# Two-layer hybrid decoder on one core: the first layer's S5 b matrices loaded later, their products moved to GpSimd, and three small reorderings

## What is computed

```
h = rms_norm(x);  proj = h @ w_in            # 1024 x 6424, split by columns
mixer A: S5 diagonal state space, 32 groups x 16 channels, 64 complex states
    bb = f * b           (f from lambda and step; b: 32 x 64 x 16, real and imaginary)
    x = u @ bb;  h = scan(a, x);  y = Re(c @ h) + d*u;  gelu, glu
mixer B: compressed / selected / window attention with rotary positions (rope)
mixer C: stick-breaking attention (softplus, running sums, exp)
x = x + (sum of gates * (mixer @ w_branch)) @ w_out
x = x + (silu(conv3(h @ up_gate)) * conv3(h @ up_value)) @ w_down
```

## Time and profile before

| | |
|---|---|
| median of 3 runs | 948.28 us (947.02 to 948.35) |
| the profiled execution | 950.34 us, its span 948.6 us, mean granted clock 0.996 |
| PE busy | 925.0 us, 98% of the span |
| DVE, ACT, POOL busy | 708.3, 592.2 and 289.2 us |
| idle before PE's work, the largest by releaser | DVE wl L1733 5.7 us, DMA at the start 3.2 us, DVE wl (at L959) 2.4 us |

### The profile page before, as it was taken

The page is one execution under the profiler, slowest core; times in us unless marked ns, Lnnn a source line. Parts: engine busy times, 40 slices in busy tenths (PEclk is TensorE's granted clock), DMA queues, the critical chain, the costliest instruction groups (busy, mean ns, idle before and its releaser), DMA issues.

```text
span 948.6 us, 16008 instructions
## 1 busy us (share of the span) xinstructions
PE 925.0 (98%) x5839; PEld 776.7 (82%) x5839; DVE 708.3 (75%) x1131; ACT 592.2 (62%) x956; POOL 289.2 (30%) x226
## 2 busy tenths in 40 slices
PE   8899999999999999999999999999999999999997
PEld 6889777777778888888879987777787788888886
DVE  6799967665667887898864977766657687777777
ACT  7445776768455765666665467677664566566655
POOL 0433324351420568467101413443316001010010
PEclk9999999999999999999999999999999999999999
DMA  9993433453554755556449844433645456556551
GB/s 221 247 269 98 147 123 132 132 150 129 167 176 138 219 192 193 177 185 213 139 123 264 233 154 134 133 117 106 180 131 178 133 178 207 193 177 205 191 179 45
DMA packets 139559, 159.09 MB, mean 168 GB/s; under 512 B 17153, under 2 KB 106089, under 8 KB 139498
## 3 DMA queue, kind: packets, MB, share of 16 engines
q1 hardware_dynamic: 137960, 156.44, 53.6%
q10 hardware_dynamic: 1538, 1.84, 0.7%
HBM read 154.33 MB, written 1.05 MB: 164 GB/s over the span
## 4 chain that ended last, share of the span: by engine, by line
PE 78%; DVE 9%; ACT 4%; SPq 3%; DMA 2%; issue 2%; ACTq 1%; POOL 0%; DVEq 0%; PEldq 0%; POOLq 0%
PE pj L801 57%; PE bX L801 7%; PE bA L801 6%; PE bB L801 4%; DVE wl L1733 3%; DMA ring<-in_w_in 2%; PE pj L1069 1%; ACT wh L1390 1%; SPq L618 1%; PE pj L1165 1%; SPq L671 1%; DVE gate L1758 1%; DVE s5a L1960 1%; DVE h L1765 1%; SPq L615 1%
## 5 line engine op out<-in xcount | busy, mean ns | idle before, releaser
L1733 DVE TENSOR_TENSOR wl<-ring,wh 128x1024 fp32r<-128x1024 f32 (+1 forms) x276 | 361.4, 1311 | 96.0 <-ACT wh L1390 94.8
L1390 ACT ACTIVATE wh<-ring 128x1024 fp32r<-128x1024 f32 (+1 forms) x276 | 288.2, 1045 | 154.4 <-PE pj L801 112.0
L801 PE MATMUL pj<-h,wh 128*128 128x256 f32 (+1 forms) x1376 | 296.6, 339 | 6.0 <-DVE wl L1733 5.0
L801 PE MATMUL pj<-wh,h 128*128 128x512 f32 (+1 forms) x832 | 259.6, 394 | 2.4 <-DVE h L1765 0.8
L801 PEld LDWEIGHTS pj<-h,wh 128*128 128x128 f32 x1376 | 230.6, 191 | 32.8 <-issue 7.0
L801 PE MATMUL pj<-h,wl 128*128 128x256 f32 x1024 | 189.0, 283 | 0.0
L801 PEld LDWEIGHTS pj<-wh,h 128*128 128x128 f32 x832 | 148.4, 188 | 41.5 <-issue 7.3
L801 PEld LDWEIGHTS pj<-h,wl 128*128 128x128 f32 x1024 | 157.6, 191 | 6.5
L801 PE MATMUL pj<-wl,h 128*128 128x512 f32 (+1 forms) x416 | 159.7, 384 | 0.0
L2422 POOL TENSOR_TENSOR work<-work 128x512 f32<-128x512 f32 x20 | 41.1, 2056 | 260.8 <-DVE work L2198 199.0
L801 PEld LDWEIGHTS pj<-wl,h 128*128 128x128 f32 x416 | 78.1, 188 | 16.3
(11 more groups left out here) (305 smaller groups left out, 1228.8 us busy)
## 6 DMA issues: line engine op xcount, KB each, us to landing
ring<-in_ffn_w_up SPq DMA_DIRECT2D x44, 1024.0 KB, 5.1
ring<-in_w_in SPq DMA_DIRECT2D x40, 1024.0 KB, 5.1
ring<-in_ffn_w_down SPq DMA_DIRECT2D x22, 1024.0 KB, 5.0
ring<-in_w_in SPq DMA_DIRECT2D x16, 512.0 KB, 5.5
ring<-in_w_branch SPq DMA_DIRECT2D x8, 1024.0 KB, 5.3
ring<-in_w_out SPq DMA_DIRECT2D x8, 1024.0 KB, 5.1
ring<-in_w_branch SPq DMA_DIRECT2D x8, 512.0 KB, 6.5
ring<-in_w_in SPq DMA_DIRECT2D x8, 256.0 KB, 3.4
```

The source lines that it names most:

```text
L801: return nc.tensor.matmul(o, a, b, start=start, stop=stop, skip_group_check=True)
L1390: A(dst, src, ACT.Copy).then_inc(w_hi.sem, 1)
L1733: TT(dst, src, hi.bitcast(F32), ALU.subtract).then_inc(w_lo.sem, 1)
```

## The change

- **Loading.** The two b matrices leave `load_mats` and get a semaphore of their own. In the first layer they are issued behind chunk 6. The rows stay behind chunk 5. What waited for six matrices now waits for four.
- **Making bb.** DVE's `s5_b` goes. POOL first does all four rope cosines, then `spread_b` (which waits for the b matrices), the products, the sums and the second spread, in one run. `s5_c`, `s5_b` and `s5_direct` on PE, the copies out on ACT, `s5_diagonal` on DVE and `s5_carried` on POOL move one slot earlier.
- **Last feed-forward step.** `ah` and `al` are made in two halves of 256 columns, with a semaphore count each; PE waits for the second before its second piece.
- **Start of the second layer.** The split of piece 1 moves behind the second `x_down` and `turned_lo`.
- **Slot 35.** The third softplus moves between the two gate copies.

```diff
-S5_C, S5_B = 2, (3, 4)
+S5_C, S5_B = 1, (2, 3)
+B_LATE, ROWS_LATE = 6, 5
...
+            def load_b(l):
+                for r, w in enumerate((ssm_b_re, ssm_b_im)):
+                    sp.dma_start(bnat[:, r], row(w, l).rearrange("l (t w) p i -> (w p) (l t) i", w=2))\
+                        .then_inc(b_in.sem, b_in.up(16))
+
             def load_mats(l):
-                for r, w in enumerate((ssm_b_re, ssm_b_im)):
-                    mat_in(bnat[:, r], row(w, l).rearrange("l (t w) p i -> (w p) (l t) i", w=2))
...
                 for i in range(5, C_FFN):
                     load(l, i)
-                    if l == 0 and i == 5:
+                    if l == 0 and i == B_LATE:
+                        load_b(0)
+                    if l == 0 and i == ROWS_LATE:
                         sp.wait_ge(setup.sem, 5)
                         load_rows(0)
...
                         if t == 0 and k:
+                            pe.wait_ge(a_split.sem, a_split.at(l, STEPS + 1))
                             pe.wait_ge(w_lo.sem, w_lo.at(l, s + 2))
...
-                    A(ah[:, :], aT[:, cc % 2, :], ACT.Copy).then_inc(a_hi.sem, 1)
-                    a_hi.made += times
+                    for c in ((slice(0, T), slice(T, 2 * T)) if cc == STEPS - 1 else (slice(0, 2 * T),)):
+                        A(ah[:, c], aT[:, cc % 2, c], ACT.Copy).then_inc(a_hi.sem, 1)
+                        a_hi.made += times
...
                     x_down(l - 1, 1, 0)
                     turned_lo(l, 1, 0, 0, 0)
-                    split_lo(l, 1)
                     x_down(l - 1, 1, 1)
                     turned_lo(l, 2, 0, 1, JC)
+                    split_lo(l, 1)
...
                 split_lo(l, 8)
-                if l == 0:
-                    s5_b()
                 split_lo(l, 9)
...
                             nc.vector.tensor_copy(gates[:, 0, t, half(1)], pj[t][:, :])\
                                 .then_inc(unit_out[n % 2].sem, unit_out[n % 2].up())
+                            if t == 0:
+                                sb_softplus(SB_P[q + 1])
+                    if q in SB_P and q != GATE_LATE + 1:
+                        sb_softplus(SB_P[q])
...
             for l in range(DEPTH):
                 cos_b = kon[:, K_COS:K_COS + T].rearrange("p (o t) -> p o t", o=1)
-                if l == 0:
-                    g.wait_ge(b_made.sem, 1)
-                    g.wait_ge(consts_in.sem, 16)
-                    spread(bb, l, 0).then_inc(bx_ready.sem, bx_ready.up())
-                    products_ab(l)
-                    sums_ab()
                 for n, dst in enumerate((kr[:, 0:2, :], kr[:, 2:3, :], qr[:, 0:2, :], qr[:, 2:4, :])):
...
-                    if l == 0 and n == 1:
-                        spread_ab(l)
+
+                if l == 0:
+                    spread_b(l)
+                    products_ab(l)
+                    sums_ab()
+                    spread_ab(l)
```

More of the change, by code:

```diff
@@ L400, in build @@
         rows_in = sem("rows_in", 16 * 11)
-        mats_in = sem("mats_in", 16 * 6)
+        b_in = sem("b_in", 16 * 2)
+        mats_in = sem("mats_in", 16 * 4)
         params_free = sem("params_free", 1, 1)
@@ L431, in build @@
         bx_ready = sem("bx_ready", 2)
-        b_made = sem("b_made")
         cx_ready = sem("cx_ready", 2)
@@ L492, in build @@
         a_ready = sem("a_ready", STEPS)
-        a_hi = sem("a_hi", STEPS)
-        a_split = sem("a_split", STEPS, 2)
+        a_hi = sem("a_hi", STEPS + 1)
+        a_split = sem("a_split", STEPS + 1, 2)
         down_done = sem("down_done", 4)
@@ L774, in _ @@
                     load_rows(l + 1)
+                    load_b(l + 1)
                     load_mats(l + 1)
@@ L1393, in spread_c @@
             def spread_c():
-                a.wait_ge(mats_in.sem, mats_in.at(0, 16 * 6))
+                a.wait_ge(mats_in.sem, mats_in.at(0, 16 * 4))
                 a.wait_ge(consts_in.sem, 16)
@@ L1880, in table @@
                     stepped(TT(tn[:, :, n:2 * n], tn[:, :, n:2 * n], turned_both[:, 0], ALU.add))
[L1882 to L1889, removed]
             for l in range(DEPTH):
@@ L2084, in s5_scan, with sb_softplus @@
                     ins.then_inc(g5_ready.sem, g5_ready.up())
+                def sb_softplus(k):
+                    v.wait_ge(z_ln.sem, z_ln.at(l, k + 1))
+                    if k:
+                        v.wait_ge(r_done.sem, r_done.at(l, k))
+                    for e in range(2):
+                        ins = STT(sbp[:, e, 0:384], (bA, bB)[e][:, 0:384], 0.0, sbw[k % 2][:, e, 0:384], ALU.max, ALU.add)
+                    ins.then_inc(z_sp.sem, z_sp.up())
                 if l:
@@ L2232, in ffn_step @@
                         split_lo(l, ffn_piece(1) + 3)
-                    v.wait_ge(a_hi.sem, a_hi.at(l, cc + 1) + turn * 2)
-                    TT(al[:, :], aT[:, cc % 2, :], ah[:, :].bitcast(F32), ALU.subtract).then_inc(a_split.sem, 1)
-                    a_split.made += times
+                    for n, c in enumerate((slice(0, T), slice(T, 2 * T)) if cc == STEPS - 1 else (slice(0, 2 * T),)):
+                        v.wait_ge(a_hi.sem, a_hi.at(l, cc + 1 + n) + turn * 2)
+                        TT(al[:, c], aT[:, cc % 2, c], ah[:, c].bitcast(F32), ALU.subtract).then_inc(a_split.sem, 1)
+                        a_split.made += times
                     if cc == STEPS - 1:
@@ L2270, in spread_c @@
             def spread_c(l):
-                g.wait_ge(mats_in.sem, mats_in.at(l, 16 * 6))
+                g.wait_ge(mats_in.sem, mats_in.at(l, 16 * 4))
                 for c, mask in enumerate((K_PAR, K_NPAR)):
@@ L2291, in spread_b @@
                 g.wait_ge(turns_ready.sem, 1)
+                g.wait_ge(b_in.sem, b_in.at(l, 16 * 2))
                 TT(bb[:, 0], bnat[:, 0], f, ALU.mult)
```

## The result

The changed kernel takes 950.32 us (median of 11 runs, 948.93 to 951.94); the kernel before, run beside it, 948.18 (11 runs, 947.02 to 949.77). The ratio is 1.0022, 95% interval 1.0012 to 1.0031: some 2 us slower, which is little, but the interval does not hold 1. Forecast were 949.3 us, 1.0 us slower, and a range of 944.0 to 953.5. The profiled execution took 951.42 us, its span 949.7; it lies 1.1 above its median, and that of before 2.1 above its own, so the two traces differ by 1.1 us where the medians differ by 2.1.

What follows compares the result with a forecast made beforehand. PE is busy 925.0 of 948.6 us; the first layer waits for chunks until about 45 us, then DVE is full. Terms +2.6 (first layer) and -1.6 (small edits) gave +1.0: 949.3 us, range 944.0 to 953.5.

Steps and rivals of the forecast that it cites:

- Loading, chunks 4 and 5: First layer's loads: chunk 4 some 4 us sooner (bounds 1.0 and 6.4), chunk 5 4 to 4.5 us sooner.
- Loading, chunk 7: First layer, b now ahead of chunk 7: its data about 46.7, unit 5's swap at 46.8, 3.5 us sooner.
- The chain: POOL's 18 first-layer operations behind the fourth cosine: start at 55.3, take 19 us (bounds 12 and 22).
- DVE's loss to it: First layer: DVE loses 8.2 us to POOL's 18 simultaneous operations (bounds 2 and 12.0).
- The sum: First layer: DVE's last rope step 5.3 us sooner, 8.2 lost less 0.3; PE's piece 22 2.6 us later, at 95.6.
- The waits on the way: First layer, PE loses its lead in two waits: about 2 us for DVE's blocks, 4 us for piece 19.
- the forecast's own case: Whole kernel: +1.0 us, median 949.3 us, own range 946.5 to 952; chance 0.50.
- The small edits: Both layers: `al` in halves -0.4, softplus and mask -0.8, second layer's start -0.4; together -1.6 us.
- Rival 1: First layer: DVE loses only 2 us to POOL's chain, so the lead reaches the end; 943.4 us, chance 0.25.
- Rival 2: First layer: DVE loses whole operations, 12.0 us, and PE's 4 us wait brings half clock; 954.2 us, chance 0.18.
- Rival 3: First layer's loads: chunk 4 gains only 1 us, chunk 7 loses as much; 952.1 us, chance 0.07.

Runs made afterwards that it cites:

- e8: The changed kernel with the b matrices issued behind chunk 7 instead of chunk 6; 949.00 us, ratio 1.0013 to the kernel before.
- e11: The changed kernel with POOL's two spreads writing into scratch and `bx` given to PE early (first layer's b products left out); 950.94 us, 1.0030 of the kernel before.
- e1: The kernel before with only the three small edits, loading and S5 chain unchanged; 946.03 us, ratio 0.9979 to the kernel before.
- e9: The changed kernel with 30 matmuls that nobody reads set ahead of piece 19 in the first layer; 951.37 us, ratio 1.0040 to the kernel before.
- e4: The changed kernel with the chain's users on PE one slot later, as before the change; 952.50 us, ratio 1.0046 to the kernel before.

## Why the prediction was right, and where two of its steps were not

- **Loading, chunks 4 and 5**: right. Hi parts at 27.21 and 35.44 (27.0 and 35.3 forecast); the parameter turns at 38.27, 1.1 us sooner than forecast.
- **Loading, chunk 7**: mis-sized. Piece 14 and unit 5's swap were put at 46.8 and came at 48.73, and a wait before piece 14 stayed, 1.56 us of 1.93. Moving b does not remove SP's time for it, which here lay in front of chunk 7: 5.21 us for the second matrix alone. With it DVE's last rope step started at 59.05 instead of 57.3. e8 moves b one chunk on and has 56.97.
- **The chain**: started 2.7 us later than forecast (58.00) and took 17.2 us, forecast 19 and 12 to 22.
- **DVE's loss to it**: right. From the rope step at 59.05 to the end of the chain, DVE's operations took 7.8 us more than the same ones alone (rope 0.7, two lo parts 1.2, blocks 3.0, the two on the gates 0.9, six table operations 2.1); forecast 8.2 less 0.3. The `carried` operations met four DVE operations as before and cost the same. The Trainium skill ("SBUF — State Buffer", section "SBUF: two separate sides") has the two engines exclude each other for whole instructions, which would be the 12.0 us that POOL's 18 operations take by the earlier trace rows. The trace does not agree for rows of this length: it has 7.8 us, 65% of that.
- **The sum**: 7.8 us lost less 3.56 us sooner (59.05 against 62.61) is +4.25 at piece 22, which is measured; forecast +2.6. The miss of 1.65 is the term of chunk 7: piece 14's lo part came at 49.81 for 47.8, and from there to the rope step the forecast holds.
- **The waits on the way** (2 us for the blocks, 4 for piece 19): 1.25 and 1.95 for blocks and `bx`, 3.88 for piece 19. None was what came last: e11 takes the first two away and gains nothing, and DVE does not wait longer than before in this stretch. The half clock, which the forecast's own case left out, came for 3.4 us and cost nothing in this execution.
- **The small edits**: worth more than forecast in the trace, not clearly so in time. Between the row at 202 and the end the trace gives back 3.2 us, forecast 1.6 with a bound of 2.4. `al` gave 0.4 and 0.3, the mask 0.7 in each layer (forecast 0.4 each), the start of layer 2 1.0 (forecast 0.4). Timed alone (e1) they are worth 2.0 us, interval 1.0 to 2.9, which holds the 1.6, so part of the trace's 3.2 may belong to the two executions.
- **Rivals**. Rival 1 failed by its condition, a loss of only 2 us. That its 943.4 is also the time of the kernel without the chain (943.42) is chance: there the rope step is 3.2 us sooner and nothing is lost, in the rival it was 5.3 less 2. Rival 2 had the half clock right, 3.4 us at 83.7, but not its price, nor the lock in full. Rival 3 is out: b's place is worth 2.6 us.

So the total, +1.0 forecast and +2.1 measured, is better than its steps, and that is luck: by the traces two errors of 1.6 us have opposite signs. By the timed halves the loading and the chain together cost 5.1 us (3.9 to 6.4) where 2.6 were forecast, and the small edits made up for some of it.

## To carry to other kernels

Before moving work to POOL, ask for DVE's busy share in the stretch where it will run, not where it ran: beside the 12 operations that POOL did before, DVE still waited 0.8 to 2.1 us for each of its next four pieces, so what it lost was waiting time; the 18 now cost 7.8 us, since DVE has no wait there. (No run took the early chain away, so its own price is not measured.) A slow DMA issue that is moved is not removed; list what stands behind it in its new place. And a change that bundles a cleverly staged part with some trivial edits should be timed in halves: here the trivial half alone is the better kernel.

## What the runs showed of the hardware

A short wait of PE can cost more than its row shows. The mask's wait stands as 0.40 us, yet its layer lost 0.7. The starts of the matmuls tell why (before, then after):

```profile
222.06 0.39 PE L801 MATMUL pj<-wl,h 128*128 128x512 f32 x1
222.84 1.14 PE L801 MATMUL bA<-kr,kon 128*128 128x256 f32 x6 [0.40 <-POOL kr L2393]
```
```profile
226.34 0.39 PE L808 MATMUL pj<-wl,h 128*128 128x512 f32 x1
226.57 1.04 PE L808 MATMUL bA<-kr,kon 128*128 128x256 f32 x6
```

From start to start it is 0.78 us with the wait and 0.23 without: 0.55 lost, since without a wait the row of the one matmul overlaps that of the next by 0.16, and the group behind the wait takes 0.10 more. That is 0.65 of the 0.7. Small waits should be costed from start to start.

The half clock is not bound to one wait's length. It came behind 1.93 us in the kernel before, behind 3.88 and not 1.95 in the changed one, behind 2.53 in e9, and about a wait of 7.89 us in e4 it lasted 10.2 us and began before the wait's end.
